# Prompt attention: transposing the probability blocks by a product with a diagonal of reciprocal sums that GpSimd builds

## The reference

```python
def attend(q, ks, vs, valid):
    B, T, H, Dh = q.shape
    qg = q.reshape(B, T, B_KV_HEADS, H // B_KV_HEADS, Dh)
    s = jnp.einsum('btngd,btknd->btngk', qg, ks).astype(jnp.float32) * ATTN_SCALE
    s = jnp.where(valid[:, :, None, None, :], s, -jnp.inf)
    p = jax.nn.softmax(s, axis=-1).astype(vs.dtype)
    o = jnp.einsum('btngk,btknd->btngd', p, vs)
    return o.reshape(B, T, H * Dh)
```

## Time and profile before

| | us |
|---|---|
| median of 3 runs | 1565.89 |
| lowest and highest of them | 1559.14, 1566.51 |
| the profiled execution | 1561.62 |
| its span, first to last instruction | 1559.4 |
| prompt attention in it, from the first exponential to the last write | 130.03 |

### The profile page before, as it was taken

The page is one execution under the profiler, slowest core; times in us unless marked ns, Lnnn a source line. Parts: engine busy times, 40 slices in busy tenths (PEclk is TensorE's granted clock), DMA queues, the critical chain, the costliest instruction groups (busy, mean ns, idle before and its releaser), DMA issues. The chain is left out here.

```text
span 1559.4 us, 25014 instructions
## 1 busy us (share of the span) xinstructions
PE 1414.2 (91%) x9464; PEld 671.2 (43%) x9464; DVE 570.0 (37%) x1266; ACT 372.2 (24%) x827; POOL 326.5 (21%) x495
## 2 busy tenths in 40 slices
PE   5989999999999899997289999999999999999955
PEld 2644444444466644453234444444444444444421
DVE  1246999970355448435810111011111011100129
ACT  1334555311466431111011111111111111111114
POOL 0217544596200014322000000000000000000037
PEclk8999999999899999998589999999999999999978
DMA  8808211221121163301869999999999999999845
GB/s 316 308 17 274 67 62 61 88 88 61 29 79 40 46 188 109 108 29 53 333 239 388 378 405 406 405 403 407 407 403 400 407 407 405 397 402 397 317 150 197
DMA packets 96366, 377.30 MB, mean 242 GB/s; under 512 B 19567, under 2 KB 37039, under 8 KB 82988
## 3 DMA queue, kind: packets, MB, share of 16 engines
q1 hardware_dynamic: 72924, 319.15, 53.0%
q10 hardware_dynamic: 16384, 32.52, 6.1%
q0 software_dynamic: 6992, 24.78, 5.1%
HBM read 340.59 MB, written 35.81 MB: 241 GB/s over the span
## 5 line engine op out<-in xcount | busy, mean ns | idle before, releaser
L1894 PE MATMUL psum<-wgu,xgT 128*32 128x256 f32 (+1 forms) x3840 | 428.7, 453 | 5.5 <-DMA wgu<-in_w_up_dram 4.6
L1894 PEld LDWEIGHTS psum<-wgu,xgT 128*32 128x32 f32 (+1 forms) x3840 | 170.6, 119 | 261.4 <-issue 212.3
L678 PE MATMUL psum<-w_sb,mixT 128*128 128x512 f32 x512 | 232.2, 607 | 10.4 <-ACT u L873 8.0
L1903 PE MATMUL psum<-wd,hidT 128*32 128x256 f32 (+1 forms) x1920 | 220.7, 454 | 0.0
L678 PEld LDWEIGHTS psum<-w_sb,mixT 128*128 128x128 f32 x512 | 96.6, 194 | 135.1 <-issue 113.5
L1943 POOL DMA_INDIRECT xg<-h_dram,tokens x33 | 30.4, 922 | 548.1 <-PE psum L1886 499.6
L1903 PEld LDWEIGHTS psum<-wd,hidT 128*32 128x32 f32 (+1 forms) x1920 | 79.7, 118 | 127.5 <-issue 101.0
L2057 DVE TENSOR_TENSOR hid<-silu,psum 128x256 f32<-128x256 f32 x40 | 16.9, 422 | 282.7 <-ACT silu L2003 282.7
L1453 PE MATMUL psum<-w_o,mixT 128*128 128x512 f32 x256 | 111.6, 594 | 1.1 <-PEq L1165 1.1
L980 DVE TENSOR_SCALAR_CACHE_REDUCE above<-bias,cand 128x384 int8<-128x384 f32 (+3 forms) x128 | 108.3, 846 | 4.6
L2003 ACT ACTIVATE silu<-psum 128x256 f32<-128x256 f32 x40 | 15.4, 384 | 325.5 <-PE psum L1894 325.5
(11 more groups left out here) (375 smaller groups left out, 1597.9 us busy)
## 6 DMA issues: line engine op xcount, KB each, us to landing
wgu<-in_w_gate_dram SPq DMA_DIRECT2D x40, 2048.0 KB, 17.7
wgu<-in_w_up_dram SPq DMA_DIRECT2D x40, 2048.0 KB, 22.7
wd<-in_w_down_dram SPq DMA_DIRECT2D x40, 2048.0 KB, 23.3
ada_b<-in_w_ada_dram ACTq DMA_DIRECT2D x16, 1024.0 KB, 4.9
ys_dram<-yy ACTq DMA_DIRECT2D x80, 128.0 KB, 8.4
ys_dram<-zero SPq DMA_DIRECT2D x22, 384.0 KB, 4.7
ada_a<-in_w_ada_dram SPq DMA_DIRECT2D x4, 2048.0 KB, 15.7
w_sb<-in_w_in_dram SPq DMA_DIRECT2D x4, 2048.0 KB, 10.1
```

Of the source, the lines that this page charges most:

```text
L678: last = nc.tensor.matmul(bank[2 + n % 2], mixT[:, k, t * P:(t + 1) * P], w_sb[:, k, n0:n0 + 512], start=(k == 0), stop=(k == DC - 1))
L1894: last = nc.tensor.matmul(out[m * j:m * j + m, 0:2 * w], xgT[:, b, k, first:first + m], wgu[:, b, :, k, w * j:w * j + w], start=(k == 0), ...
L1903: last = nc.tensor.matmul(out[m * j:m * j + m, 0:w], hT(k), wd[:, b, k, w * j:w * j + w], start=(k == 0), stop=(k == KD - 1))
```

## The change

The sums divide the probabilities already when these are transposed. In place of the transposition of a block, TensorE makes a product of the block with a diagonal matrix that holds the reciprocals of the sums: the block is the stationary operand, the diagonal rdiag the moving one. GpSimd builds the diagonals: for each pair it waits for both exponentials, raises the two sums to the power -1, waits for that, and multiplies the identity by either reciprocal. There are six diagonals, for three pairs. TensorE waits for the diagonal in place of the exponential. The reciprocals on VectorE, the four products with rden, ScalarE's copy to rb go, and VectorE's multiplication becomes a copy out of PSUM. rdiag takes the place of rb in SBUF, and the table of constants gets two columns of -1.

```diff
         "one": np.ones((P, 1)),
+        "minusone": np.full((P, 2), -1.0),
...
-        rb = at_room("rb", W0 + 60 * KB, [P, 2, P])
+        rdiag = at_room("rdiag", W0 + 60 * KB, [P, 6, P])
...
                     gate(TILES)
+                    for p in range(NPAIR):
+                        pool.wait_ge(b_exp, 2 * p + 2)
+                        g.tensor_tensor(rden[:, 2 * p:2 * p + 2], den[:, 2 * p:2 * p + 2], c("minusone"), ALU.pow).then_inc(b_rd, 1)
+                        pool.wait_ge(b_rd, p + 1)
+                        for b in range(2):
+                            e = 2 * p + b
+                            if p >= 3:
+                                pool.wait_ge(b_trf, BTRN[("pT", p - 3, b, pair(p - 3)[0] // 4)] + 1)
+                            g.tensor_scalar(rdiag[:, e % 6, :], c("ident"), rden[:, e:e + 1], None, ALU.mult).then_inc(b_dg, 1)
...
                         for col, src in parts:
-                            last = nc.tensor.transpose(bank[BTB[n % 3]][:, col:col + P], src, c("ident"))
+                            if key[0] == "pT":
+                                last = nc.tensor.matmul(bank[BTB[n % 3]][:, col:col + P], src, rdiag[:, (2 * key[1] + key[2]) % 6, :], start=True, stop=True)
+                            else:
+                                last = nc.tensor.transpose(bank[BTB[n % 3]][:, col:col + P], src, c("ident"))
                         last.then_inc(b_trf, 1)
...
                             for b in range(2):
-                                pe.wait_ge(b_exp, 2 * p + b + 1)
+                                pe.wait_ge(b_dg, 2 * p + b + 1)
...
-                            if half == 1:
-                                pe.wait_ge(b_rd, q + 1)
-                                for n in range(2):
-                                    for b in range(2):
-                                        e = 4 * q + 2 * n + b
-                                        last = nc.tensor.matmul(bank[7][64 * b:64 * b + 64, (2 + n) * P:(3 + n) * P],
-                                                                rden[:, e:e + 1].to_broadcast([P, HD]), c("ident"), start=True, stop=True)
+                            if half == (1 if cut <= t else 0):
                                 last.then_inc(b_pv, 1)
...
-                        elif kind == "pv" and i == 1:
-                            act.wait_ge(b_pv, t + 1)
-                            if t >= 1:
-                                act.wait_ge(b_o, t)
-                            s.activation(rb[:, :, :], bank[7][:, 2 * P:4 * P].rearrange("p (i n) -> p i n", i=2), ACT.Copy).then_inc(b_rbe, 1)
...
-                            if i == 1:
-                                dve.wait_ge(b_exp, 2 * p + 2)
-                                v.reciprocal(rden[:, 4 * q:4 * q + 4], den[:, 4 * q:4 * q + 4]).then_inc(b_rd, 1)
...
-                            dve.wait_ge(b_rbe, q + 1)
-                            v.tensor_tensor(mixT[:, 4 + 2 * j:6 + 2 * j, t * P:(t + 1) * P], bank[7][:, 0:2 * P].rearrange("p (i n) -> p i n", i=2),
-                                            rb[:, :, :], ALU.mult).then_inc(b_o, 1)
+                            dve.wait_ge(b_pv, q + 1)
+                            v.tensor_copy(mixT[:, 4 + 2 * j:6 + 2 * j, t * P:(t + 1) * P], bank[7][:, 0:2 * P].rearrange("p (i n) -> p i n", i=2)).then_inc(b_o, 1)
```

More of the change, by code:

```diff
@@ L296, in step_kernel @@
             b_rd = stage_sem("b_rd")
+            b_dg = stage_sem("b_dg")
             b_pv = stage_sem("b_pv")
-            b_rbe = stage_sem("b_rbe")
             b_o = stage_sem("b_o")
@@ L764, in _ @@
                                     kv = 2 * j + b
-                                    nc.tensor.matmul(bank[7][64 * b:64 * b + 64, 0:2 * P], v_nat[:, k, kv * HD:(kv + 1) * HD],
+                                    last = nc.tensor.matmul(bank[7][64 * b:64 * b + 64, 0:2 * P], v_nat[:, k, kv * HD:(kv + 1) * HD],
                                                      pT[:, q % 2, b, k, :, :], start=(k == 0), stop=(k == t))
-                            if half == 1:
-                                pe.wait_ge(b_rd, q + 1)
-                                for n in range(2):
-                                    for b in range(2):
-                                        e = 4 * q + 2 * n + b
-                                        last = nc.tensor.matmul(bank[7][64 * b:64 * b + 64, (2 + n) * P:(3 + n) * P],
-                                                                rden[:, e:e + 1].to_broadcast([P, HD]), c("ident"), start=True, stop=True)
+                            if half == (1 if cut <= t else 0):
                                 last.then_inc(b_pv, 1)
```

## The result

The changed kernel took 1609.38 us in the median of four runs (1608.10 to 1614.44), the kernel before 1564.63 beside it: a ratio of 1.031, with a 95% interval of 1.0283 to 1.0337. The prediction was 1608 in a range of 1583 to 1640. The profiled execution took 1608.1 us for a span of 1606.3, against 1561.62 and 1559.4 before.

What follows compares the result with a forecast made beforehand. TensorE was taken to bound the prompt attention. Loop-paced tiles up to t = 5 and TensorE-paced ones from t = 6 summed to 174.6 us against 130.0, 44.6 more, giving 1606.2; the answer was 1608, range 1583 to 1640.

Steps and rivals of the forecast that it cites:

- What bounds the kernel: Prompt attention, 130.03 us: TensorE, 93% to 100% busy per row; a closed loop through ScalarE's copy is no longer.
- TensorE loses: Prompt attention: 64 broadcast products go, 8.6 us; 0.9 us less for each of the two last groups.
- TensorE gains: Prompt attention blocks: product of two records replaces one-record transposition, 0.22 us for 0.11; 31.7 us over 288 blocks.
- The rival on that factor: Prompt attention: a product costs four transpositions, TensorE paces from t = 5; some 100 us more, 1661; chance 0.04.
- GpSimd's chain: Between exponentials and products: power 0.72 us, multiplication 0.30, plus semaphores; enters the loop of each pair.
- X: Delay from GpSimd's work and semaphores before a pair's first product: 1.41 us, bounds 1.19 and 2.59.
- The loop: Prompt attention: exponentials, GpSimd, products, copy set the pace up to t = 5; stage 174.6 us against 130.0.
- From t = 6 TensorE, by a hair: Widest query tiles: TensorE's own work, 7.2 us a pair at t = 7, just exceeds the loop's 7.1.
- Behind the stage: After prompt attention: nothing takes up the delay, so the 44.6 us go to the end.
- The rival on the power: GpSimd (rival B): power costs nearly its eight-column price, 0.95 us more; some 30 us, 1636; chance 0.15.
- The case that only the records count: Prompt attention: GpSimd's chain is hidden, only TensorE's records count; 21 us more, 1583; chance 0.06.
- A: Prompt attention: both terms, records and chain, as worked out; 1606, bounds 1596 to 1622; chance 0.60.

Runs made afterwards that it cites:

- The two orders on ScalarE: Changed kernel, next exponentials ahead of ScalarE's copies everywhere: 1611.26 us; ahead up to the fourth tile, then between the two heads' copies: 1589.70 us.
- the two on VectorE: Changed kernel, VectorE building reciprocals and diagonals in GpSimd's place: behind its mask of the next pair 1662.57 us, ahead of that mask 1583.69 us.
- the run without either: Changed kernel with blocks transposed by the identity, no GpSimd diagonals and no division: 1602.99 us, stage 121.0 us.
- the doubled power: Changed kernel with GpSimd's power done twice in each pair (two powers): 1641.17 us, stage 208.0 us.
- the run that makes it so: Changed kernel with the product taking the identity, no GpSimd diagonals and no division: 1629.26 us, stage 148.8 us.
- the division by transfer: Kernel before, groups 4 to 14 divided by GpSimd, with reciprocals sent to memory and loaded back: 1607.67 us, stage 175.7 us.

## Why the prediction was right

The direction, the size and the mechanism held. By its own steps:

**What bounds the kernel** was TensorE, and the closed loop of exponentials, transposition and copy was there, with little slack at the narrow tiles and some 1.2 us a pair at the seventh, where only 1.3 of 6.3 us of chain came through. The two orders on ScalarE and the two on VectorE show it by opening and closing it.

**TensorE loses** 8.6 and 1.8 us by the prediction, 10.4 in all; 9.0 by the run without either.

**TensorE gains** 31.7 us by two records a block; 576 records came, 32 in 3.65 us of weight loads, 0.228 us a block where 0.22 was taken. The stage paid 27.8 us: TensorE's busy time grew by 29.6, and 1.9 of that filled idle time. The factor of four for fp32 in the Trainium skill, TensorE: Matmul & The Clock Gate, section Terms, does not show at 128 columns: 16 blocks went from 2.00 us to 3.84, a factor of 1.9. The rival on that factor falls.

**GpSimd's chain** was the mis-sized term, in two parts of which one takes back half of the other. The power took 0.72 us as worked out. The multiplication took 0.61 where the prediction took 0.30, "near the copy, since one tensor is read"; it lies above the two-operand sum (0.53), so the nearest row was the other bound. The three semaphore steps took 0.09, 0.09 and 0.07 where 0.39 was counted. X came to 1.57, not 1.41. The Trainium skill, GPSIMD Engine Reference, section Engine selection, puts one-input operations on GpSimd at roughly line rate beside VectorE; here the same multiplication takes 0.61 us on GpSimd, and two take 0.48 on VectorE, so this trace does not bear it out.

**The loop** summed to 174.6 us and measured 180.8. At t = 4 to 7 each tile is 1.0 us longer than summed, 0.25 a pair: in the pair shown 0.16 are X, and 0.08 the nine products with the time to the copy, 2.31 us where 9 x 0.22 + 0.25 = 2.23 was counted. The narrow tiles were off to both sides, 13.8, 14.7, 16.9 and 20.1 against 13.2, 16.0, 16.0 and 18.1: the second was counted at half clock and ran at 0.96, and the fourth ran at 0.92 where 1.00 was counted. That fits the signs of the two misses; no run changes the clock alone. The lower clock did not hold to t = 3 as that rival had it.

**From t = 6 TensorE, by a hair:** the hair is on the other side. The seventh tile takes 28.01 us, where TensorE alone needs 26.70 with the same records, 0.33 a pair less. It idles 3.4 us for GpSimd in five places from 522 to 586, and the doubled power came through nearly whole. The waits of single loads reach 2.6 us where "under 1 us each" was expected, 30 of them in place of 32; the average wait of a product, 23.1/25, is 0.92.

**Behind the stage** nothing absorbs it, as forecast. The prediction named stages after 538 that shrink as a sign that it is wrong, and one stretch did, from 200.4 to 197.3 us; but in the twelve experiments it lasts 196.7 to 198.7, whatever the stage took, so it is the one execution of the kernel before that stands apart. That the total came within 1.4 us of 1608 owes something to chance: the stage was 6.2 us longer than summed, and the unchanged stretch behind it 3.1 us shorter in the profiled execution; and the 1608 itself was put between two bases.

**The rival on the power** (0.95 us more) falls with 0.72 measured. The case that only the records count was priced at 21 us over the kernel before, and the run that makes it so measured 18.7. A's bounds of 1596 to 1622 have no working beside them; X at its own bounds, by the 30 us for 0.95 of rival B, gives 1599 to 1643. None of the other rivals has support left.

## What to carry to other kernels

Before an operation is put between two engines that hand work to each other, look for the loop: if the engine that must start the next round has its work queued behind a copy of this one, what is added to the hand-over is paid each round, however idle the new engine is, as soon as the round is longer than the bound engine's own work. Ask first what stands ahead of the operation in the new engine's queue, and what that waits for; the same three instructions on VectorE cost 75 us more or less by their place. And price an operation that replaces a cheap one in all its repetitions: sixteen groups of products cost 9 us, and folding the division into 288 transpositions cost 28 before any wait.

## What the runs showed of the hardware

A power on GpSimd takes 0.57, 0.72 and 1.67 us at 1, 2 and 8 columns (exponents of -0.5, -1 and -0.5): about 0.16 us a column and 0.4 fixed. A multiplication of 128x128 by a scalar per partition takes it 0.61 us, longer than a sum of two such tiles (0.53). VectorE's reciprocal takes 0.17 us at 2 and at 4 columns and 1.74 at 256, 6.3 ns a column between the last two.

A write of 2 KB that turns 128x4 values into four rows in memory takes 8.5 us to land in the median, where a load of 128 KB took 2.1 in the kernel before; in the kernel that sends such writes the same page loads took 4.2. Why they took longer is not shown.

The mean granted clock of the stage, between the lower level of 0.50 (1.2 GHz) and the upper of 1.00 (2.4 GHz), was lowest in the three kernels in which TensorE was idle most. These are their windows of the stage: two powers, the diagonal behind VectorE's mask, and the division by transfer:

```profile
407.97:616.01 208.04, 163.73 (x1080) 113.31 (x1080) 75.62 (x188) 79.38 (x185) 83.51 (x128) 0.91 0.10 26
```

```profile
407.29:638.39 231.10, 172.24 (x1080) 122.43 (x1080) 93.68 (x284) 79.51 (x185) 0.00 (x0) 0.88 0.09 24
```

```profile
408.50:584.20 175.70, 130.94 (x832) 76.52 (x832) 69.27 (x193) 82.41 (x201) 29.52 (x44) 0.86 0.17 39
```

It was 0.96 before and 0.95 after. The first two have the same 1080 records as the changed kernel's 156.50 us, and TensorE was busy 163.73 and 172.24 with them. In the widest tile the same 258 records take 33.14 us in the changed kernel and 33.16 with the identity, both at 1.00, 35.06 with two powers at 0.96 and 38.06 with the diagonal behind the mask at 0.89. So waits can make the work behind them slower too, which adds to their price. Not every wait does: with two powers TensorE was idle 6.9 of 22.16 us in the fourth tile, at 1.00.
